# Down weights read as 8 KB row pairs, with a column step of two in the transposes before them: a two-layer decoder trunk on one core

## The reference, cut to what matters

```python
D_FF = 2816; N_EXPERTS = 8; TOP_K = 2; D_FF_EXPERT = 3584

def swiglu(x, w_gate, w_up, w_down):
    return (jax.nn.silu(x @ w_gate) * (x @ w_up)) @ w_down

# layer 0
h = h + swiglu(rms_norm(h, e_norm_ffn[j]), e_ffn_gate[j], e_ffn_up[j], e_ffn_down[j])   # down: (2816, 1024)
# layer 1: every token goes to 2 of 8 experts
for e in range(N_EXPERTS):
    out = out + gates[..., e:e+1] * swiglu(x, w_gate[e], w_up[e], w_down[e])            # down: (3584, 1024)
```

## Time and profile before

| | us |
|---|---|
| median of 3 runs | 1434.71 (1434.13 to 1434.95) |
| span of the profiled execution, first to last instruction | 1433.4 |
| TensorE matmul busy | 1418.3 (99%) |
| TensorE weight load busy | 1195.2 (83%) |
| DVE busy | 1148.5 (80%) |
| ACT busy | 966.5 (67%) |

### The profile page before, as it was taken

The page is one execution under the profiler, slowest core; times in us unless marked ns, Lnnn a source line. Parts: engine busy times, 40 slices in busy tenths (PEclk is TensorE's granted clock), DMA queues, the critical chain, the costliest instruction groups (busy, mean ns, idle before and its releaser), DMA issues.

```text
span 1433.4 us, 19865 instructions
## 1 busy us (share of the span) xinstructions
PE 1418.3 (99%) x7061; PEld 1195.2 (83%) x7061; DVE 1148.5 (80%) x987; ACT 966.5 (67%) x895; POOL 88.5 (6%) x96
## 2 busy tenths in 40 slices
PE   9999999999999999999999999999999999999997
PEld 8988888889997888888888888888888888888885
DVE  5776544567658889888988988988898898898996
ACT  5555434346547777777777877777777787777775
POOL 2000000000004750000000000000000000002000
PEclk9999999999999999999999999999999999999999
DMA  9758655564543999999999999999999999999990
GB/s 321 251 176 318 221 180 193 188 235 148 171 153 145 399 395 394 395 394 382 369 393 371 374 394 380 358 397 392 363 389 393 379 360 394 377 351 397 396 368 30
DMA packets 197798, 454.59 MB, mean 317 GB/s; under 512 B 7481, under 2 KB 28997, under 8 KB 197758
## 3 DMA queue, kind: packets, MB, share of 16 engines
q1 hardware_dynamic: 190944, 429.94, 81.7%
q0 software_dynamic: 5040, 17.92, 3.4%
q10 hardware_dynamic: 1774, 6.17, 1.1%
HBM read 439.30 MB, written 14.70 MB: 317 GB/s over the span
## 4 chain that ended last, share of the span: by engine, by line
PE 96%; DVE 2%; ACT 1%; DMA 0%; issue 0%; POOL 0%; DVEq 0%; ACTq 0%; POOLq 0%
PE bank L1525 21%; PE bank L991 15%; PE bank L1506 14%; PE bank L1510 14%; PE bank L1513 14%; PE bank L1025 5%; PE bank L1299 4%; PE bank L1492 2%; PE bank L1186 1%; PE bank L1091 1%; ACT w_hi L565 1%; PE bank L1111 0%; DMA work<-in_o_norm_ple 0%; DVE w_lo L1599 0%; PE bank L1473 0%; PE bank L1141 0%
## 5 line engine op out<-in xcount | busy, mean ns | idle before, releaser
L1599 DVE TENSOR_TENSOR w_lo<-raw,w_hi 128x2048 fp32r<-128x2048 f32 x406 | 926.5, 2291 | 208.5 <-ACT w_hi L565 207.2
L565 ACT ACTIVATE w_hi<-raw 128x2048 fp32r<-128x2048 f32 x406 | 779.7, 1921 | 343.5 <-PE bank L1513 145.5
L1506 PE MATMUL bank<-w_hi,x_hi 128*128 128x512 f32 x896 | 244.8, 395 | 0.0
L1510 PE MATMUL bank<-w_hi,x_lo 128*128 128x512 f32 x896 | 240.1, 390 | 0.0
L1513 PE MATMUL bank<-w_lo,x_hi 128*128 128x512 f32 x896 | 239.7, 389 | 0.0
L1510 PEld LDWEIGHTS bank<-w_hi,x_lo 128*128 128x128 f32 x896 | 168.3, 188 | 36.0
L1513 PEld LDWEIGHTS bank<-w_lo,x_hi 128*128 128x128 f32 x896 | 168.2, 188 | 35.2 <-DVE w_lo L1599 0.2
L1506 PEld LDWEIGHTS bank<-w_hi,x_hi 128*128 128x128 f32 x896 | 164.2, 188 | 30.6
L1525 PE MATMUL bank<-w_hi,m_lo 128*128 128x512 f32 x448 | 121.2, 390 | 0.0
L1525 PE MATMUL bank<-w_lo,m_hi 128*128 128x512 f32 x448 | 121.0, 389 | 0.0
L1525 PE MATMUL bank<-w_hi,m_hi 128*128 128x512 f32 x448 | 120.6, 391 | 0.0
(11 more groups left out here) (277 smaller groups left out, 1347.6 us busy)
## 6 DMA issues: line engine op xcount, KB each, us to landing
raw<-in_o_exp_gate SPq DMA_DIRECT2D x112, 1024.0 KB, 7.4
raw<-in_o_exp_up SPq DMA_DIRECT2D x112, 1024.0 KB, 8.0
raw<-in_o_exp_down SPq DMA_DIRECT2D x112, 1024.0 KB, 7.8
raw<-in_o_w_qkv SPq DMA_DIRECT2D x12, 1024.0 KB, 5.1
raw<-in_e_ffn_gate SPq DMA_DIRECT2D x11, 1024.0 KB, 5.2
raw<-in_e_ffn_up SPq DMA_DIRECT2D x11, 1024.0 KB, 5.2
raw<-in_e_ffn_down SPq DMA_DIRECT2D x11, 1024.0 KB, 5.0
raw<-in_e_w_in SPq DMA_DIRECT2D x9, 1024.0 KB, 16.6
```

Source lines behind the costliest of these rows:

```text
L565: act.activation(w_hi[:, slot % SPLIT], raw[:, slot], ACT.Copy).then_inc(hi_made, 1)
L1506: pe.matmul(dst, x_hi[:, c + kk, 0:P], hi[:, kk], start=(c, kk) == (0, 0), stop=False)
L1510: pe.matmul(dst, x_lo[:, c + kk, 0:P], hi[:, kk], start=False, stop=False)
L1599: ve.tensor_tensor(w_lo[:, slot % SPLIT], raw[:, slot], w_hi[:, slot % SPLIT], ALU.subtract).then_inc(lo_made, 1)
```

## The change

The two views of the down weights now put rows 256 i + 2 p and 256 i + 2 p + 1 into partition p, chunk 0 and chunk 1. Both rows are neighbours in memory, so a partition's part of a tile is one run of 8 KB in place of two of 4 KB. To match, chunk c of a turned block must hold hidden columns 256 (c // 2) + c % 2, then every second one, 128 in all. `chunk_of(c)` gives that slice, and the transposes of `ffn_turn` and `turn` read with it. Nothing else changes: the same tiles are loaded in the same order, with the same waits, and every instruction has the same number of elements.

```diff
+        def chunk_of(c):
+
+            first = c // 2 * 2 * P
+            return slice(first + c % 2, first + 2 * P, 2)
+
...
-            down_v = e_ffn_down[0].rearrange("(i c p) n -> i p c n", p=P, c=2)
+            down_v = e_ffn_down[0].rearrange("(i p c) n -> i p c n", p=P, c=2)
...
-            ed = o_exp_down[0].rearrange("e (i c p) n -> e i p c n", p=P, c=2)
+            ed = o_exp_down[0].rearrange("e (i p c) n -> e i p c n", p=P, c=2)
...
# ffn_turn
-                        mm = pe.transpose(bank[banks[t]][:, c * P:(c + 1) * P], ffn_hid[:, t, c * P:(c + 1) * P], ident)
+                        mm = pe.transpose(bank[banks[t]][:, c * P:(c + 1) * P], ffn_hid[:, t, chunk_of(c)], ident)
...
# turn
-                    mm = pe.transpose(bank[2][:, c * P:(c + 1) * P], hid_sb[:, c * P:(c + 1) * P], ident)
+                    mm = pe.transpose(bank[2][:, c * P:(c + 1) * P], hid_sb[:, chunk_of(c)], ident)
```

## The result

The changed kernel takes 1438.04 us (median of 9 runs, 1437.22 to 1438.50) against 1434.61 us for the kernel before (9 runs beside it, 1434.06 to 1435.14): 3.4 us slower, a ratio of 1.0024 with a 95% interval of 1.0015 to 1.0034. The profiled execution took 1437.57 us and has a span of 1435.8 us. The runs of both kernels read 1.7 to 1.8 us more than their own spans; the 1.3 us of the prediction was the distance from the profiled span to the median of other runs. The forecast went by the median, so this does not move it.

What follows compares the result with a forecast made beforehand. TensorE's instruction steps were taken as the bound, with weights arriving early. The profiled span of 1433.4 us plus 0 for loads and 0 for transposes, plus 1.3 us to the runs' median, gave 1434.7 us; 8-in-10 range 1433.2 to 1438.2.

Steps and rivals of the forecast that it cites:

- What bounds the kernel: Whole kernel: TensorE's instruction steps set the time; weights arrive early, a down tile's load ending 4.6 us before ACT wants it.
- The loads: 123 down tiles in 8 KB pieces: 15,744 fewer packets, time effect taken as 0, bounds -0.25 to +4.2 us.
- B: Rival, last job: 8 KB pieces make the full DMA slip further behind, time up to 1438.9 us; chance 0.03.
- C: Rival, expert blocks: DMA is the real bound and larger pieces raise its rate, 34 us faster, 1401 us; chance 0.04.
- D: Rival, down loads: pieces stay at 4 KB, time same as forecast, packets stay 190,944; within the 0.84 for no change.
- The transposes: 268 transposes on TensorE's path: the strided weight load taken to cost 0, from zero up to 34 us at quarter rate.
- half the read rate: Transposes' weight load at 198 ns: at most 13 ns a transpose, 3.5 us in all, 1438.2 us.
- rival A: 268 transposes: strided weight load slower, 1438.2 us at half rate, 1469 at a quarter; chance 0.09, half rate or less 0.06.
- no change: Whole kernel: time within about 0.2% (2.9 us) of before, likeliest 1434.7 us; chance 0.84.

Runs made afterwards that it cites:

- loads_only: Against the kernel before: only the 8 KB down-weight loads, transposes still reading contiguous columns; 1434.15 us, ratio 0.9999.
- strided_only: Against the kernel before: only the transposes' column step of two, down weights still loaded in 4 KB pieces; 1437.76 us, ratio 1.0024.
- inter_strided: The changed kernel with an expert turn's four transposes placed singly, each ahead of a 512-column matmul; 1437.25 us, 1.0022 against the kernel before.
- the pairs: Kernel before, first gate and up pass streaming its moving operand in runs of two columns, then two skipped; 1638.12 us, ratio 1.1421.
- mov_quads: Kernel before, first gate and up pass streaming its moving operand in runs of four columns, then four skipped; 1445.21 us, ratio 1.0074.

## Why the prediction was wrong

**What bounds the kernel**: right. TensorE's steps set the time before and after, and loads_only shows that the stream of weights has the slack that the timeline gave it.

**The loads**: right, 0 taken, and -0.3 us measured with an interval of -1.4 to +1.1 us (1434.15 against 1434.45 us), with the packet count forecast to the packet. Rivals B, C and D fall with it.

**The transposes**: this step failed, and it was the choice inside it, not the bounds: the term was put at 0 us, and it measured 3.4 us (3.3 us with the columns alone, in strided_only). The working for half the read rate said: a weight load of 198 ns, 13 ns a transpose, 3.5 us, a time of 1438.2 us, rival A with 0.06. Measured are 204 to 209 ns, 3.4 us, 1438.04 us. That the two totals agree so well is in part luck. The 13 ns were the difference to the step of another kind of matmul, and the working put all of them on the transpose itself. The step of a transpose in a row of eight went from 0.87 / 8 = 109 to 0.95 / 8 = 119 ns, four in a turn from 0.44 to 0.47 us, about 8 ns each; the rest is in the plain matmuls behind the turn, which the prediction did not count. The time lay inside the range only because the range had been drawn out to this case; the likeliest outcome, no change, had been given 0.84.

Why zero was taken and should not have been. I argued that a plain load reads at one column per 0.87 ns and a transposing one per 0.46 ns, and that both fit their step. The first half is true, but the fit was between a 192 ns load and a step of 122 ns. No row showed a load of that length under a step of 109 ns. My own sum had 118 ns of reading against a step of 109 ns, which does not fit. The row nearest to the case of half rate was the 122 ns of the earlier trace rows, and taking its difference to 109 ns would have been the price. Under a 227 ns matmul the longer load is mostly hidden, as inter_strided shows.

What was open was whether the rate would halve at all. There I leaned on a sentence of the Trainium skill ("SBUF — State Buffer", Specifications, the row on cachelines): 16-byte lines, and two accesses to a line give full speed, so a float32 step of two should be free. The runs here speak against the second part. Two of a line's four float32 are read by the step of two and by the pairs, and both halve the rate of the moving side (452 and 450 ns in place of 227). The step of two also halves that of the transposing load (59 to some 124 ns of reading, if 80 ns are fixed as the prediction estimated). The size of 16 bytes agrees: runs of four restore the rate of the moving side to 232 ns. No run tried them on the stationary side. A step of four, one value per line, costs no more than a step of two in the load.

## What to carry to other kernels

A layout change that gives DMA larger pieces is paid for where the compute engine reads across it. Ask of both sides whether they stand on the path: here DMA had 4.6 us of slack per tile and could return nothing, while the transposes were bare on TensorE. Put such a permutation on an engine with slack and with no price for the step (DVE's product took 680 ns either way), and keep the moving operand of a float32r matmul in whole runs of 16 bytes: a step of two there doubled the matmul. For the stationary operand the runs show only that neighbouring columns load fastest. When the working for one bound gives a number that just fails to fit under its cover, as 118 ns under 109 ns did here, that bound deserves far more than a chance of 0.06.

## What the runs showed of the hardware that I had not expected

A moving float32r operand of 512 columns goes from a step of 227 ns to 452 to 460 ns as soon as part of each 16-byte run is skipped, and it makes little difference how much. A transposing weight load goes from 139 to 204 ns with a step of two or four. A plain float32r weight load, already the slower one at 188 ns, goes to 193 ns only, but that still cost 6 ns on each matmul of 512 columns. The transposed operand is float32 and the plain one float32r; whether the type or the transposing makes the difference between these two loads was not tested. Contiguous transposes of 128 columns keep their step of about 109 ns behind another transpose and behind a 512-column matmul alike; strided ones have 119 ns in a row of eight. What sets the 109 ns, what the matmuls behind a strided load lose their time to, and what sets the 12 ns of mov_quads, no run here tells.
